# Banded attention beside gated projections: the fourth projection step of every even unit moves behind the second value product

## The chip, the cores and the metric

The kernel runs on one core of one Trainium2 chip. The metric is the device time of one execution in microseconds; the time before is the median of three executions. A core has five engines with a queue of instructions each, and each queue is worked off in the order in which the program wrote it: TensorE (PE, with its weight loads shown apart as PEld), VectorE (DVE), ScalarE (ACT), GpSimd (POOL) and SyncE (SP, here only for DMAs).

## The reference, cut to what matters

One encoder layer of 1024 tokens and 1024 channels. A normalised input is projected; the columns go to two head groups. Group A is banded attention: 8 query heads, 2 key-value heads, and a block of 128 queries sees its own block of keys and the two beside it.

```python
scores = jnp.einsum('bnqgrd,bnkgd->bngrqk', qb, kb).astype(jnp.float32)
scores = scores * (HEAD_DIM ** -0.5)
...
scores = jnp.where(mask[None, :, None, None], scores + bias[None, None], -jnp.inf)
...
m = jnp.maximum(jnp.max(scores, axis=-1, keepdims=True), sink_l)
p = jnp.exp(scores - m)
denom = jnp.sum(p, axis=-1, keepdims=True) + jnp.exp(sink_l - m)
probs = (p / denom).astype(v.dtype)
out = jnp.einsum('bngrqk,bnkgd->bnqgrd', probs, vb)
...
ya = ya * jax.nn.silu(ga)
```

Group B is dense latent attention with its own gate `gb`. Both go through one output projection, a residual sum and a last norm.

## The kernel before, in words

Every engine's program is written out by hand, and semaphores tie them together. The stage around the change is the banded attention, at some 229 to 345 us of the profile. It runs over 16 **units**: unit u is query block n = u // 2 and key-value group g = u % 2, with its four query heads. A loop over s runs from 0 to 16 on each engine; step s works on the scores of unit s and on the value products of unit s - 1 (the text says "unit s" for step s of this loop). The keys of a unit are 3 blocks of 128 (2 blocks for units 0, 1, 14 and 15), called c0, c1 and c2 below.

In step s:

- TensorE makes the scores of unit s (`scores_w`, 8 matmuls, L1601 and L1602, banks 0 to 3), then transposes the probabilities of unit s - 1 for c0 and c1 (`turn_w`, 4 transposes each, L1613, banks 4 and 5), makes the value product of c0 (`pv_w`, 2 matmuls, L1623 and L1624, bank 7), transposes c2, and makes the value products of c1 and c2.
- VectorE takes the negated row maxima of the four heads (`max_w`, L1181), adds the two halves of the output of unit s - 2 (`o_w_sum`, L1219), makes the low part of each transposed block (`pT_w_lo`, L1209), the reciprocal of the sums (`recip_w`, L1195 and L1196), and scales one head's probabilities (`probs_w`, L1203).
- ScalarE copies the lower half of the output (`o_w_lo`, L865), makes the exponentials (`exp_w`, L848, and `exp_sink_w`, L853) and the high part of each transposed block (`pT_w_hi`, L859).
- GpSimd scales the other three heads' probabilities (`probs_w`, L580) and multiplies by the gate (`gate_w`, L591).

Between these, TensorE has work that waits for nothing in this loop: the gated projection jobs. Job g is one 128 x 512 tile of the gate columns, summed over 8 steps; a step k is three matmuls (`three`, L1425 to L1427: high by high, low by high, high by low) into bank 6. `beside(s)` gives each unit four steps of one job: odd units the steps 0 to 3, even units the steps 4 to 7, so that **a job ends in an even unit**. Its last matmul raises `s_g`; ScalarE then takes the tanh from the bank into `Y` (`evac_g`, L841), and VectorE joins the two in `Y` (`evac_g`, L1168). Both stand at the end of step s in their engine's queue, on VectorE right ahead of the first `max_w` of step s + 1:

```python
                if live:
                    probs_w(s)
                if s % 2 == 0:
                    evac_g(N_WIN_JOB + s // 2)
```

A value product waits for `s_wTl`, VectorE's low part of its block (L1209); the scores of a unit wait for the row maxima of the unit before; `max_w` waits for the scores. The first two of the four steps of a unit stand between the transposes and the product of c0; the change is about the other two, "the third" and "the fourth". In even units the fourth is step 7, which ends the job.

Of the kernel before, what the change touches and what calls it, by code (L numbers as in the profile page):

```python
# [71 lines left out]
def encoder(nc, x, norm_mix, w_in, attn_sink, q_a_norm, w_uq, kv_a_norm, w_ukv, w_out, final_norm,  # L72
# [8 lines left out]
    with ExitStack() as ctx:  # L81
# [196 lines left out]
        def beside(s):  # L278


            if s == 0:
                return N_WIN_JOB, range(KT)
            return N_WIN_JOB + (s + 1) // 2, range(4 * ((s + 1) % 2), 4 * ((s + 1) % 2) + 4)
# [4 lines left out]
        def w_keys(u):  # L288
            n = u // GROUPS
            return range(max(n - 1, 0), min(n + 2, NT))  # L290

        W_UNITS = NT * GROUPS
# [1129 lines left out]
        def _(pe):  # L1422
# [155 lines left out]
            def gated(g, ks):  # L1578
                m, cols = g // 2, slice(g % 2 * HALF, (g % 2 + 1) * HALF)
                if ks[0] == 0:  # L1580
                    pe.wait_ge(s_wr, m + 1)
                    if g < 2:
                        wait_up_copied(pe, UP_LAST[g])
                    else:
                        pe.wait_ge(s_ge, g if g > N_WIN_JOB else g - 1)
                for k in ks:
                    last = three(ps[:, g_bank(g), :], w_hi[:, m % 2, k, :], w_lo[:, m % 2, k, :],
                                 hT_hi[:, k, cols], hT_lo[:, k, cols], k == 0, k == KT - 1)
                if ks[-1] == KT - 1:
                    last.then_inc(s_g, 1)  # L1590

            def scores_w(u):
                n, g, keys = u // GROUPS, u % GROUPS, w_keys(u)
                k0, w = keys[0] * P, len(keys) * P
                if u == 0:
                    wait_up_copied(pe, len(UP) - 1)
                for r in range(REP):
                    if u >= 1:
                        pe.wait_ge(s_wm, REP * (u - 1) + r + 1)
                    q = q_st[:, REP * g + r, n * P:(n + 1) * P]  # L1600
                    nc.tensor.matmul(ps[:, r, 0:w], q, k_hi2[:, g, k0:k0 + w], start=True, stop=False)  # L1601
                    nc.tensor.matmul(ps[:, r, 0:w], q, k_lo2[:, g, k0:k0 + w], start=False,  # L1602
                                     stop=True).then_inc(s_ws, 1)

            def turn_w(u, i):
                c = W_FIRST[u] + i
                if i == 0:
                    pe.wait_ge(s_wp, POOL_R * (u + 1))
                    pe.wait_ge(s_wpd, u + 1)
                if c >= 2:  # L1610
                    pe.wait_ge(s_wTl, c - 1)
                for r in range(REP):
                    last = nc.tensor.transpose(ps[:, 4 + c % 2, r * P:(r + 1) * P],  # L1613
                                               p_w[:, u % 2, r, i * P:(i + 1) * P], ident[:, :])
                last.then_inc(s_wT, 1)

            def pv_w(u, i):
                c, keys = W_FIRST[u] + i, w_keys(u)
                if i == 0:
                    pe.wait_ge(s_wo, u) if u else pe.wait_ge(s_ge, N_WIN_JOB)  # L1620
                pe.wait_ge(s_wTl, c + 1)
                v = vA[:, keys[i], u % GROUPS, :]
                nc.tensor.matmul(ps[:, 7, :], v, pT_wh[:, c % 2, :], start=(i == 0), stop=False)  # L1623
                nc.tensor.matmul(ps[:, 7, :], v, pT_wl[:, c % 2, :], start=False,  # L1624
                                 stop=(i == len(keys) - 1)).then_inc(s_wpv, 1)
# [29 lines left out]
            for s in range(W_UNITS + 1):  # L1655
                g, ks = beside(s)
                n = len(w_keys(s - 1)) if s >= 1 else 0
                if s < W_UNITS:
                    scores_w(s)
                if s == W_UNITS:  # L1660
                    gated(g, ks[:len(ks) // 2])
                    ks = ks[len(ks) // 2:]
                for i in range(min(n, 2)):
                    turn_w(s - 1, i)
                if 2 <= s < W_UNITS or s == 0:
                    gated(g, ks[:len(ks) // 2])
                    ks = ks[len(ks) // 2:]
                else:
                    gated(g, ks)
                if n:  # L1670
                    pv_w(s - 1, 0)
                    if n > 2:
                        turn_w(s - 1, 2)
                before = len(ks) if s % 2 == 0 else len(ks) // 2
                if 2 <= s < W_UNITS or s == 0:
                    gated(g, ks[:before])
                if n:
                    pv_w(s - 1, 1)
                if before < len(ks) and s >= 2:
                    gated(g, ks[before:])  # L1680
                if n > 2:
                    pv_w(s - 1, 2)
# [140 lines left out]
```

## Time and profile before

| what | value |
| --- | --- |
| median of three executions | 638.8 us (638.74 to 638.92) |
| the profiled execution, its own time | 639.14 us |
| span of the profiled execution | 636.6 us |
| busy: TensorE matmul / weight load | 626.3 us (98%) / 526.7 us (83%) |
| busy: VectorE / ScalarE / GpSimd | 438.5 us (69%) / 355.4 us (56%) / 315.9 us (50%) |
| mean granted TensorE clock | 0.999 |
| share of TensorE in the chain that ended last | 94% |

The span runs from the first to the last instruction; the device time holds 2.5 us more that lie around it. A matmul's length in the timeline overlaps that of the next, so TensorE's pace is read from the distance of two starts, and its lost time from starts that lie further apart than that. An "idle before" is time in which an engine had nothing, with the instruction that released it behind the arrow.

### The profile page before, as it was taken

How to read it: one execution, taken by the hardware profiler on the slowest of the kernel's cores; microseconds unless marked ns; L12 is line 12 of the kernel's file. 1: busy time of each engine (PE TensorE's matmuls, PEld its weight loads, DVE VectorE, ACT ScalarE, POOL GpSimd, SP SyncE). 2: the span in 40 equal slices, each digit the busy share in tenths (PEclk: the TensorE clock that was granted, in tenths of full speed). 3: DMA queues.
4: the chain of work that ended last, by engine and by line, in shares of the span. 5: the costliest groups of instructions: out<-in, count | busy, mean ns of one | idle time of the engine just before them, and what ended most of it. 6: DMA issues, size and time to landing. Idle time of an engine off the chain costs nothing.

```text
span 636.6 us, 9352 instructions
## 1 busy us (share of the span) xinstructions
PE 626.3 (98%) x3267; PEld 526.7 (83%) x3267; DVE 438.5 (69%) x850; ACT 355.4 (56%) x765; POOL 315.9 (50%) x304
## 2 busy tenths in 40 slices
PE   8999999999999999999999999999999999999996
PEld 7888888888888887888887788888888888888885
DVE  4673326333444448899998788888888888799695
ACT  5662222223333237777776777777777778542563
POOL 2724004404656433644545776877876788610710
PEclk9999999999999999999999999999999999999999
DMA  6540016365676520100015011010010403399033
GB/s 222 188 166 1 1 38 234 134 256 184 227 250 229 190 64 1 34 1 1 10 42 175 0 43 43 1 41 19 24 43 0 141 1 134 108 339 346 0 142 123
DMA packets 41662, 66.80 MB, mean 105 GB/s; under 512 B 3496, under 2 KB 18352, under 8 KB 41488
## 3 DMA queue, kind: packets, MB, share of 16 engines
q1 hardware_dynamic: 41472, 65.95, 31.2%
q8 instruction: 26, 0.43, 0.3%
q10 hardware_dynamic: 144, 0.26, 0.1%
q14 instruction: 20, 0.16, 0.1%
HBM read 46.15 MB, written 20.05 MB: 104 GB/s over the span
## 4 chain that ended last, share of the span: by engine, by line
PE 94%; DVE 2%; ACT 2%; issue 1%; POOL 1%; POOLq 0%; ACTq 0%
PE ps L1427 21%; PE ps L1425 21%; PE ps L1426 21%; PE ps L1696 9%; PE ps L1712 5%; PE ps L1713 5%; PE ps L1613 3%; PE ps L1623 2%; PE ps L1624 1%; PE ps L1437 1%; PE ps L1602 1%; PE ps L1601 1%; PE ps L1477 1%; PE ps L1465 1%; POOL p_w L580 1%
## 5 line engine op out<-in xcount | busy, mean ns | idle before, releaser
L654 POOL TENSOR_SCALAR p_b<-p_b,stat 128x1024 f32<-128x1024 f32 x64 | 72.1, 1126 | 51.2 <-DVE stat L1280 50.7
L928 ACT ACTIVATE pT_hi<-ps 128x512 fp32r<-128x512 f32 x128 | 69.6, 596 | 45.4 <-PE ps L1696 45.4
L1285 DVE TENSOR_TENSOR pT_lo<-ps,pT_hi 128x512 fp32r<-128x512 f32 x128 | 81.8, 680 | 5.2 <-ACT pT_hi L928 5.1
L1275 DVE TENSOR_REDUCE stat<-ps 128x1 f32<-128x1024 f32 x64 | 77.7, 1214 | 10.7 <-PE ps L1427 10.4
L1425 PE MATMUL ps<-hT_hi,w_hi 128*128 128x512 f32 x208 | 83.9, 403 | 0.0
L1427 PE MATMUL ps<-hT_hi,w_lo 128*128 128x512 f32 x208 | 81.4, 391 | 0.0
L1426 PE MATMUL ps<-hT_lo,w_hi 128*128 128x512 f32 x208 | 81.0, 390 | 0.0
L917 ACT ACTIVATE p_b<-ps,stat 128x1024 f32<-128x1024 f32 x64 | 71.5, 1117 | 10.4 <-DVE stat L1275 10.3
L1696 PEld LDWEIGHTS ps<-ident,p_b 128*128 128x128 f32 x512 | 59.9, 141 | 8.9 <-issue 0.5
L1696 PE MATMUL ps<-ident,p_b 128*128 128x128 f32 x512 | 66.5, 273 | 0.1
L580 POOL TENSOR_SCALAR p_w<-p_w,stat 128x384 f32<-128x384 f32 (+1 forms) x48 | 27.8, 596 | 59.5 <-DVE stat L1196 59.5
L1712 PE MATMUL ps<-pT_hi,vB 128*128 128x512 f32 x128 | 55.2, 431 | 0.9 <-DVE Y L1168 0.9
L1713 PE MATMUL ps<-pT_lo,vB 128*128 128x512 f32 x128 | 50.3, 393 | 0.0
L1426 PE MATMUL ps<-k_lo,q_hi 96*128 96x512 f32 x126 | 49.7, 395 | 0.0
L1427 PE MATMUL ps<-k_hi,q_lo 96*128 96x512 f32 x126 | 49.7, 395 | 0.0
L1425 PE MATMUL ps<-k_hi,q_hi 96*128 96x512 f32 x126 | 49.5, 393 | 0.0
L518 POOL TENSOR_SCALAR w_hi<-w_raw 128x1024 fp32r<-128x1024 f32 x13 | 14.1, 1081 | 65.6 <-PE ps L1427 65.6
L1427 PEld LDWEIGHTS ps<-hT_hi,w_lo 128*128 128x128 f32 x208 | 39.0, 188 | 8.4
L1425 PEld LDWEIGHTS ps<-hT_hi,w_hi 128*128 128x128 f32 x208 | 39.1, 188 | 7.5 <-issue 0.4
L1425 PE MATMUL ps<-wn_hi,hT_hi 128*128 128x288 f32 (+1 forms) x128 | 45.1, 352 | 0.0
L1426 PEld LDWEIGHTS ps<-hT_lo,w_hi 128*128 128x128 f32 x208 | 39.2, 188 | 7.1
L1427 PE MATMUL ps<-wn_hi,hT_lo 128*128 128x288 f32 (+1 forms) x128 | 44.1, 344 | 0.0
(219 smaller groups left out, 1525.6 us busy)
## 6 DMA issues: line engine op xcount, KB each, us to landing
w_raw<-w_in SPq DMA_DIRECT2D x13, 512.0 KB, 4.5
x_in<-x SPq DMA_DIRECT2D x8, 512.0 KB, 3.5
wt_raw<-w_out SPq DMA_DIRECT2D x8, 512.0 KB, 4.6
t_scratch<-wt_hi SPq DMA_DIRECT2D x16, 256.0 KB, 2.4
t_scratch<-wt_lo SPq DMA_DIRECT2D x16, 256.0 KB, 2.6
wn_raw<-w_in SPq DMA_DIRECT2D x8, 336.0 KB, 3.5
q_nope_scratch<-stage SPq DMA_DIRECT2D x8, 256.0 KB, 3.1
k_nope_scratch<-stage SPq DMA_DIRECT2D x8, 256.0 KB, 3.3
```

The costliest lines, as they stand in the source:

```text
L580: nc.gpsimd.tensor_scalar(p_w[:, u % 2, r, 0:w], p_w[:, u % 2, r, 0:w], w_col(5, u)[:, r:r + 1], 0.5, ALU.mult, ALU.mult).then_inc(s_wp, 1)
L654: nc.gpsimd.tensor_scalar(p_b[:, (U + 1) % 4, :], p_b[:, (U + 1) % 4, :], r_b[:, U % 4:U % 4 + 1], 0.5, ALU.mult, ALU.mult).then_inc(s_bp, 1)
L917: nc.scalar.activation(p_b[:, (U + 1) % 4, :], ps[:, b:b + 2, :].rearrange("p b c -> p (b c)"), ACT.Exp, bias=nm_b[:, U % 4:U % 4 + 1], ac ...
L928: nc.scalar.activation(pT_hi[:, 1 - G % 2, 4 * a:4 * a + 4, U % 4 * P:(U % 4 + 1) * P], ps[:, 4 + a, :].rearrange("p (k c) -> p k c", c=P) ...
L1275: nc.vector.tensor_reduce(nm_b[:, U % 4:U % 4 + 1], ps[:, b:b + 2, :].rearrange("p b c -> p (b c)"), AX.X, ALU.max, negate=True).then_inc( ...
L1285: nc.vector.tensor_tensor(pT_lo[at_], ps[:, 4 + a, :].rearrange("p (k c) -> p k c", c=P), f(pT_hi[at_]), ALU.subtract).then_inc(s_bTl, 1)
L1425: nc.tensor.matmul(o, a_hi, b_hi, start=first, stop=False, skip_group_check=goes_on)
L1426: nc.tensor.matmul(o, a_hi, b_lo, start=False, stop=False, skip_group_check=goes_on)
L1427: return nc.tensor.matmul(o, a_lo, b_hi, start=False, stop=last, skip_group_check=goes_on)
L1696: last = nc.tensor.transpose(ps[:, 4 + a, k * P:(k + 1) * P], p_b[:, (U + 1) % 4, (4 * a + k) * P:(4 * a + k + 1) * P], ident[:, :])
L1712: nc.tensor.matmul(o, vB[:, 1 - hp, k, :], pT_hi[:, 1 - G % 2, k, :], start=(k == 0), stop=False)
L1713: last = nc.tensor.matmul(o, vB[:, 1 - hp, k, :], pT_lo[:, 1 - G % 2, k, :], start=False, stop=(k == NT - 1))
```

## The change

One expression that says how many of the two remaining gated steps stand ahead of the value product of c1. Before, both in even units and one in odd units; now one in each unit from 2 to 15. Units 0, 1 and 16 keep what they had. No instruction is added or removed, no DMA moves, and the queues of VectorE, ScalarE, GpSimd and SyncE stay as they were, row for row.

```diff
                     pv_w(s - 1, 0)
                     if n > 2:
                         turn_w(s - 1, 2)
-                before = len(ks) if s % 2 == 0 else len(ks) // 2
+                before = len(ks) // 2 if 2 <= s < W_UNITS else len(ks)
                 if 2 <= s < W_UNITS or s == 0:
                     gated(g, ks[:before])
                 if n:
                     pv_w(s - 1, 1)
                 if before < len(ks) and s >= 2:
                     gated(g, ks[before:])
                 if n > 2:
                     pv_w(s - 1, 2)
```

So the fourth step moves in the seven even units 2 to 14. On TensorE in unit 2, where the unit before has two key blocks, the rows are these (k_hi and k_lo by q_st are scores, hT by w the gated step, pT by vA the value product):

```order
 L1426 MATMUL ps<-hT_lo,w_hi 128x512
 L1427 MATMUL ps<-hT_hi,w_lo 128x512
-L1425 MATMUL ps<-hT_hi,w_hi 128x512
-L1426 MATMUL ps<-hT_lo,w_hi 128x512
-L1427 MATMUL ps<-hT_hi,w_lo 128x512
 L1623 MATMUL ps<-pT_wh,vA 128x512 [waits w_pT_lo]
 L1624 MATMUL ps<-pT_wl,vA 128x512
+L1425 MATMUL ps<-hT_hi,w_hi 128x512
+L1426 MATMUL ps<-hT_lo,w_hi 128x512
+L1427 MATMUL ps<-hT_hi,w_lo 128x512
 L1601 MATMUL ps<-k_hi_84,q_st 128x384 [waits w_max]
 L1602 MATMUL ps<-k_lo_85,q_st 128x384
```

The gated step that ended ahead of the product of c1 now ends right ahead of the next unit's scores.

On TensorE in unit 4, and in the same way in units 6, 8, 10, 12 and 14, where the unit before has three key blocks:

```order
 L1426 MATMUL ps<-hT_lo,w_hi 128x512
 L1427 MATMUL ps<-hT_hi,w_lo 128x512
-L1425 MATMUL ps<-hT_hi,w_hi 128x512
-L1426 MATMUL ps<-hT_lo,w_hi 128x512
-L1427 MATMUL ps<-hT_hi,w_lo 128x512
 L1623 MATMUL ps<-pT_wh,vA 128x512 [waits w_pT_lo]
 L1624 MATMUL ps<-pT_wl,vA 128x512
+L1425 MATMUL ps<-hT_hi,w_hi 128x512
+L1426 MATMUL ps<-hT_lo,w_hi 128x512
+L1427 MATMUL ps<-hT_hi,w_lo 128x512
 L1623 MATMUL ps<-pT_wh,vA 128x512 [waits w_pT_lo]
 L1624 MATMUL ps<-pT_wl,vA 128x512
```

The same step, the last of its job, now stands between the products of c1 and c2; the product of c1, with its wait for VectorE, comes three matmuls earlier.

## Rows read from the trace of the kernel before

**Rows 1.** Busy us by engine (and instructions), clock, DMA, 269 to 283 us

```profile
269.00:283.00 14.00, 13.96 (x76) 11.52 (x75) 12.66 (x35) 10.55 (x27) 4.69 (x8) 1.00 0.00 1
```

**Rows 2.** Waits in 228 to 346 us: total us, times, longest

```profile
PEld ps L1623 <- DVE pT_wl L1209: 7.4, 21, 0.6
...
DVE p_w L1181 <- PE ps L1602: 4.1, 7, 0.6
```

**Rows 3.** Timeline of unit 6 (start, length, instruction, idle before)

```profile
269.59 0.62 DVE L1181 CUSTOM_DVE_ANT_0 p_w<-distb,ps,nsink 128x384 f32<-128x384 f32 x1 [0.63 <-PE ps L1602]
...
273.47 0.68 DVE L1209 TENSOR_TENSOR pT_wl<-ps,pT_wh 128x512 fp32r<-128x512 f32 x1
...
274.63 0.40 PE L1427 MATMUL ps<-hT_hi,w_lo 128*128 128x512 f32 x1
...
274.77 0.69 DVE L1209 TENSOR_TENSOR pT_wl<-ps,pT_wh 128x512 fp32r<-128x512 f32 x1
...
274.87 0.39 PE L1623 MATMUL ps<-pT_wh,vA 128*128 128x512 f32 x1
...
275.07 0.60 ACT L841 ACTIVATE Y<-ps 128x512 f32<-128x512 f32 x1 [0.33 <-PE ps L1427]
...
275.52 0.19 PEld L1623 LDWEIGHTS ps<-pT_wh,vA 128*128 128x128 f32 x1 [0.46 <-DVE pT_wl L1209]
...
276.05 0.67 DVE L1168 SCALAR_TENSOR_TENSOR Y<-Y,ps 128x512 f32<-128x512 f32 x1
```

**Rows 4.** Timeline of unit 5

```profile
262.43 0.61 DVE L1181 CUSTOM_DVE_ANT_0 p_w<-distb,ps,nsink 128x384 f32<-128x384 f32 x1
...
263.81 0.60 ACT L859 ACTIVATE pT_wh<-ps 128x512 fp32r<-128x512 f32 x1
...
266.31 0.69 DVE L1209 TENSOR_TENSOR pT_wl<-ps,pT_wh 128x512 fp32r<-128x512 f32 x1
...
267.05 0.19 PEld L1623 LDWEIGHTS ps<-pT_wh,vA 128*128 128x128 f32 x1 [0.29 <-DVE pT_wl L1209]
...
268.08 0.40 PE L1427 MATMUL ps<-hT_hi,w_lo 128*128 128x512 f32 x1
...
268.36 0.19 PEld L1623 LDWEIGHTS ps<-pT_wh,vA 128*128 128x128 f32 x1 [0.31 <-DVE pT_wl L1209]
```

**Rows 5.** Timeline of unit 8

```profile
287.90 0.68 DVE L1209 TENSOR_TENSOR pT_wl<-ps,pT_wh 128x512 fp32r<-128x512 f32 x1
...
288.96 0.39 PE L1427 MATMUL ps<-hT_hi,w_lo 128*128 128x512 f32 x1
...
289.39 0.60 ACT L841 ACTIVATE Y<-ps 128x512 f32<-128x512 f32 x1 [0.34 <-PE ps L1427]
...
290.36 0.67 DVE L1168 SCALAR_TENSOR_TENSOR Y<-Y,ps 128x512 f32<-128x512 f32 x1
```

**Rows 6.** Timeline from unit 2 into unit 3

```profile
245.51 0.68 DVE L1209 TENSOR_TENSOR pT_wl<-ps,pT_wh 128x512 fp32r<-128x512 f32 x1
...
246.25 0.40 PE L1427 MATMUL ps<-hT_hi,w_lo 128*128 128x512 f32 x1
...
246.69 0.60 ACT L841 ACTIVATE Y<-ps 128x512 f32<-128x512 f32 x1 [0.39 <-PE ps L1427]
...
247.32 0.69 DVE L1168 SCALAR_TENSOR_TENSOR Y<-Y,ps 128x512 f32<-128x512 f32 x1 [0.16 <-ACT Y L841]
...
249.48 0.60 ACT L859 ACTIVATE pT_wh<-ps 128x512 fp32r<-128x512 f32 x1 [0.20 <-PE ps L1613]
...
250.11 0.69 DVE L1209 TENSOR_TENSOR pT_wl<-ps,pT_wh 128x512 fp32r<-128x512 f32 x1 [0.16 <-ACT pT_wh L859]
```

**Rows 7.** Timeline of unit 14

```profile
330.09 0.68 DVE L1209 TENSOR_TENSOR pT_wl<-ps,pT_wh 128x512 fp32r<-128x512 f32 x1
...
331.88 0.60 ACT L841 ACTIVATE Y<-ps 128x512 f32<-128x512 f32 x1 [0.60 <-PE ps L1427]
...
332.51 0.69 DVE L1168 SCALAR_TENSOR_TENSOR Y<-Y,ps 128x512 f32<-128x512 f32 x1
```

## Prediction

> **What bounds the kernel now.** I read the busy time of the banded stage first. Of 14 us in its middle TensorE shows 13.96 busy, VectorE 12.66, ScalarE 10.55 and GpSimd 4.69, at a granted clock of 1.00 [rows 1]. TensorE looks like the bound, but its matmuls overlap in the records, so I went on to the waits: in this stage 21 weight loads of a value product waited for VectorE's low part, and in turn 7 row maxima waited for TensorE's scores [rows 2]. Two engines that wait for each other form a ring, and the question is which pieces of it have no slack.
>
> The timeline of a pair of units answers it. In unit 5 VectorE starts its first maximum at 262.43 with no idle time ahead of it, because it came straight from other work [rows 4]; in unit 6 the first maximum at 269.59 waited 0.63 us for the scores [rows 3]. So the ring is: VectorE's maxima of an odd unit, by way of ScalarE's exponentials and high parts, to the low part of c2; TensorE's product of c2 at 268.36, which waited for just that [rows 4]; the scores of the even unit; VectorE's even unit without a gap worth naming; `evac_g` at 276.05; the next odd unit's maxima. TensorE is on it only from 268.36 to 269.59. Inside an even unit it runs beside the ring, and VectorE's `evac_g` is on it. That is the place to price.
>
> A rule of the Trainium skill bears on this choice. By Perfetto Trace Analysis, Identifying the Most-Contended Engine, matmul busy time is a bad measure, and weight-load busy time is to be set against VectorE's occupancy. Here that is 11.52 us against 12.66 [rows 1], so by the rule VectorE is the engine to guard, where the matmul row alone would name TensorE; by the rule I would go with the forecast below, by the matmul row with the first rival.
>
> **What the change moves.** Nothing is added or removed; three matmuls of 0.23 us pace change places with two, seven times. Two things follow in an even unit: the product of c1 comes three matmuls earlier and may now wait for its low part; and the last matmul of the job, on which ScalarE's tanh and then VectorE's `evac_g` wait, comes later.
>
> *Units 6 and 10.* The low part of c1 ends at 273.47 + 0.68 = 274.15 [rows 3]. TensorE would be there at 274.63 - 2 x 0.23 = 274.17, so they meet almost exactly. Unit 5 is already laid out in the new way and gives the price: low part ends at 266.31 + 0.69 = 267.00, the load follows at 267.05, and the last matmul of the fourth step starts at 268.08, thus 1.03 us behind the load [rows 4]. (At full pace these four distances would be 0.92; 0.11 is a weight load that nothing covers.) In unit 6 that makes load 274.20 and last matmul 275.23, where it was 274.63 [rows 3]: 0.60 later.
>
> ScalarE's tanh starts 0.44 behind that matmul and takes 0.60, and `evac_g` could begin 0.03 later (246.69 + 0.60 to 247.32 in rows 6), at 275.70. It began at 276.05, since VectorE was busy until then [rows 3]: 0.35 us of cover. So 0.60 - 0.35 = **0.25 us** reach VectorE. TensorE itself loses nothing: after 275.23 it is at the product of c2 at 275.46, and the low part of c2 ends at 274.77 + 0.69 = 275.46, load 275.51, as before [rows 3].
>
> *Units 4, 8 and 12.* Here the low part of c1 comes a little later: 287.90 + 0.68 = 288.58, load 288.63, last matmul 289.66 where it was 288.96, 0.70 later. The cover is 290.36 - (289.39 + 0.60 + 0.03) = 0.34, which leaves **0.36** [rows 5]. The same arithmetic on unit 4 gives 0.34 and on unit 12 0.36.
>
> *Unit 2.* The unit before has two key blocks, so there is no product of c2 to meet, and VectorE has no third low part. c1's low part ends at 245.51 + 0.68 = 246.19, load 246.24, last matmul 247.27 where it was 246.25: 1.02 later. There is no cover: `evac_g` already waited 0.16 for the tanh. In unit 3 ScalarE had 0.20 to spare ahead of its first high part, and VectorE's low part waits for that one, so 1.02 - 0.20 = **0.82** goes on [rows 6]. Bounds: the scores of unit 3 come 247.27 + 0.23 - (246.25 + 3 x 0.23) = 0.56 later in any case, which is the least; 1.02 is the most.
>
> *Unit 14.* The low part of c1 ends at 330.77, and TensorE comes there no earlier (tanh at 331.88, so the last matmul at 331.44, less 2 x 0.23) [rows 7]. So the step is later by two matmuls alone, 0.46. `evac_g` at 332.51 stood 0.03 behind the tanh's end at 332.48, without cover [rows 7]: **0.46**.
>
> *What waits behind `evac_g`.* On VectorE all maxima of the odd unit, its output sum and its low parts; behind the first maximum ScalarE's first exponential and, in its queue, the high part of c0; behind the low parts TensorE's products. In unit 5 the high part of c0 runs 263.81 to 264.41 and the load of c1's product stood 0.29 and that of c2's 0.31 for VectorE [rows 4]; I see no slack in between that would eat 0.25 us. The 0.63 us that VectorE waits in the even unit [rows 3] is no slack either: it waits for scores that TensorE makes after the late product, so it waits as long as before. No DMA is issued by the moved step, and bank 6 is needed again only behind the next unit's scores and transposes. GpSimd's last weight splits wait for jobs that ended over a unit ago.
>
> **The sum**: 0.82 + 0.34 + 0.25 + 0.36 + 0.25 + 0.36 + 0.46 = 2.84 us, on the profiled execution 639.14 + 2.84 = 641.98. That execution lies 0.34 over the median of 638.8, so I forecast 641.6 us for the median, 0.44% slower. The dense stage behind starts later by the same amount, and I take it that it gives nothing back: its first scores follow on TensorE without a pause.
>
> Bounds of what the trace does not show. Each of the five middle units could cost nothing (if VectorE's odd unit has slack that I missed) or 0.36 (the larger of the two). If the ring swallows all five, units 2 and 14 stay: 0.82 + 0.46 = 1.28, thus 640.1. Upwards: unit 2 in full 1.02, five at 0.36, unit 14 0.46, and on top in all seven an uncovered weight load of 0.11: 3.28 + 0.77 = 4.05, thus 642.8.
>
> **Rivals.**
>
> *TensorE is the bound, and the moved step fills its wait: faster.* The product of c2 in the five middle units waits: its load at 275.52 stands 0.19 behind the pace (274.87 + 2 x 0.23 = 275.33) [rows 3], and with the uncovered load of 0.11 that is 0.30 lost. The new order puts a step into it and pays 0.03 + 0.11 at the product of c1, so 0.16 would be saved five times: 0.8 us, 638.0. For it speaks the 13.96 of 14 us. Against it: the low part of c2 hangs on the exponentials, not on TensorE's matmuls of that moment, so the product can't start sooner; it decides only if that low part came 0.16 us earlier. I give it 0.05.
>
> *Swallowed: no change.* The later `evac_g` would be absorbed by slack in the odd unit, and unit 2 too. The idle times in rows 4 speak against it. 639 to 640: 0.09.
>
> *Only the ends count.* The middle units meet their cover, units 2 and 14 cost: 640.1, on the border of what can be told. 0.10.
>
> *TensorE pays too.* The wait for c1 is longer than reckoned, so that the product of c2 is late as well, by 0.11 each time or more: 642.4 and above. 0.08.
>
> *The forecast*, 641.0 to 642.3: 0.68.
>
> **Numbers.** About 0.2% (1.3 us) is what a measurement of this kernel can tell from no change. Slower than 640.1 are the forecast, the last rival and half of "only the ends": 0.81. Same: the swallowed case, half of the ends: 0.14. Faster: 0.05. The range of 8 in 10 takes in the ends and part of the bounds: 640.1 to 642.6.
>
> **What would show it.** In the changed profile: (1) in unit 6 a load of the product of c1 that waits for L1209 and starts 0.05 behind its end, and none longer than before at c2; (2) the tanh of unit 6 starting 1.52 us behind the end of the low part of c1 (275.67 against 274.15); (3) `evac_g` in all seven even units with a wait for ScalarE's tanh ahead of it, 0.25 to 0.36 in the middle; (4) the distance from one even unit's first maximum to the next 0.25 to 0.36 us longer than now; (5) the first scores of the dense stage 2.8 us later. The forecast is wrong if (3) holds and (4) does not: then the odd unit has slack. It is also wrong if the wait at c1 is longer than at unit 5.

## The result, and the profile after

The changed kernel takes 640.83 us (median of 6 runs, 640.20 to 641.15) against 638.76 us for the kernel before (6 runs, 637.81 to 638.92): ratio 1.0035, 95% interval 1.0025 to 1.0045. It is 2.07 us slower. The forecast was 641.6 us with a range of 640.1 to 642.6. The profiled execution spans 638.4 us, 1.8 more than before. Its banded stage began 0.5 us earlier than that of the profile before, so the loss within the stage is 2.3 us.

The busy times of the whole span tell nothing of it: TensorE's matmuls rose from 626.3 to 627.9 us and its weight loads fell from 526.7 to 526.0. Nor does the same stretch of 14 us as in [rows 1]:

```profile
269.00:283.00 14.00, 14.00 (x76) 11.48 (x76) 12.51 (x35) 10.56 (x27) 4.57 (x8) 1.00 0.00 1
```

TensorE now shows 14.00 of 14 us busy, and the kernel is slower. The waits of the banded stage (total us, times, longest; to be laid beside [rows 2]) say more:

```profile
ACT Y L841 <- PE ps L1427: 15.2, 10, 4.8
...
DVE Y L1168 <- ACT Y L841: 10.2, 10, 4.8
...
PEld ps L1623 <- DVE pT_wl L1209: 9.4, 27, 0.7
```

Before, the wait of `evac_g` for the tanh was this:

```profile
DVE Y L1168 <- ACT Y L841: 7.5, 4, 4.8
```

TensorE's loads waited for VectorE's low parts 27 times instead of 21, and 9.4 us instead of 7.4. ScalarE's tanh waited 15.2 us for the jobs' last matmuls instead of 10.5. VectorE's `evac_g` waited 10 times for the tanh instead of 4: all seven changed units now wait, by 1.18, 0.26, 0.17, 0.24, 0.17, 0.28 and 0.57 us, where only unit 2 did before. VectorE's wait for scores is the old one (4.1 us, 7 times). The delay comes back to TensorE one unit later: ahead of the loads of value products the view shows 3.1 us of idle time without a releaser ("issue"), 0.4 before, and all but 0.2 of it stands at the product of c0 in the odd units.

Unit 6 and the start of unit 7 after the change (start, length, instruction, idle before), to be laid beside [rows 3]:

```profile
270.20 0.62 DVE L1181 CUSTOM_DVE_ANT_0 p_w<-distb,ps,nsink 128x384 f32<-128x384 f32 x1 [0.62 <-PE ps L1602]
...
274.09 0.68 DVE L1209 TENSOR_TENSOR pT_wl<-ps,pT_wh 128x512 fp32r<-128x512 f32 x1
...
274.82 0.19 PEld L1623 LDWEIGHTS ps<-pT_wh,vA 128*128 128x128 f32 x1 [0.29 <-DVE pT_wl L1209]
...
275.85 0.40 PE L1427 MATMUL ps<-hT_hi,w_lo 128*128 128x512 f32 x1
...
276.29 0.60 ACT L841 ACTIVATE Y<-ps 128x512 f32<-128x512 f32 x1 [0.93 <-PE ps L1427]
...
276.92 0.69 DVE L1168 SCALAR_TENSOR_TENSOR Y<-Y,ps 128x512 f32<-128x512 f32 x1 [0.17 <-ACT Y L841]
...
277.52 0.60 DVE L1181 CUSTOM_DVE_ANT_0 p_w<-distb,ps,nsink 128x384 f32<-128x384 f32 x1
```

The low part of c1 ends at 274.09 + 0.68 = 274.77 and the load follows at 274.82. The last matmul of the job starts 1.03 behind it, at 275.85, the tanh at 276.29, and `evac_g` has waited 0.17 us. The first maximum stands 0.60 behind `evac_g`, and 0.30 behind the end of its scores (276.88 + 0.34 = 277.22). So `evac_g` holds the maximum, and not the scores. Nor is it ScalarE's own queue that hands the delay on, for its next exponential waits 0.67 us for that maximum. Counted from the unit's first maximum, `evac_g` starts at 6.72 us; before it was 276.05 - 269.59 = 6.46. The forecast said 0.25 later, and it is 0.26. But the unit 7 that follows is only 0.16 later.

The first maximum (first L1181) of each unit, counted from that of unit 0, gives the whole account. Before, it stands at 230.04, 269.59 and 276.75 for units 0, 6 and 7, after at 229.57, 270.20 and 277.52; "dense" is the first matmul of the dense scores (L1640; 343.12 and 344.96). What the change added by then, in us:

| at unit | 3 | 4 | 5 | 6 | 7 | 8 | 9 | 10 | 11 | 12 | 13 | 14 | 15 | dense |
| --- | --- | --- | --- | --- | --- | --- | --- | --- | --- | --- | --- | --- | --- | --- |
| after less before | 1.03 | 0.84 | 1.09 | 1.08 | 1.24 | 1.25 | 1.49 | 1.49 | 1.66 | 1.66 | 1.93 | 1.94 | 2.33 | 2.31 |

All steps stand at odd units, right behind the `evac_g` of a changed unit, and between an odd and the next even unit nothing is added; at unit 4 the spare time of unit 3 is given back, as forecast.

### The profile page after: what moved, and what is told of

Same layout as the page of the kernel before. It is cut to its first block, busy times and chain, and to the rows that moved or that the text cites. A ratio compares the mean times of both kernels' runs of the same rounds, so it can differ in the third digit from the quotient of the medians.

```text
span 638.4 us, 9352 instructions
## 1 busy us (share of the span) xinstructions
PE 627.9 (98%) x3267; PEld 526.0 (82%) x3267; DVE 438.8 (69%) x850; ACT 355.8 (56%) x765; POOL 316.6 (50%) x304
## 4 chain that ended last, share of the span: by engine, by line
PE 94%; DVE 3%; ACT 1%; issue 0%; POOL 0%; POOLq 0%; ACTq 0%
PE ps L1425 21%; PE ps L1427 21%; PE ps L1426 21%; PE ps L1696 9%; PE ps L1712 5%; PE ps L1713 5%; PE ps L1613 3%; PE ps L1623 2%; PE ps L1624 1%; PE ps L1602 1%; PE ps L1601 1%; PE ps L1437 1%; PE ps L1477 1%; DVE p_w L1181 1%; DVE pT_wl L1209 1%; PE ps L1465 1%
## 5 line engine op out<-in xcount | busy, mean ns | idle before, releaser
L1275 DVE TENSOR_REDUCE stat<-ps 128x1 f32<-128x1024 f32 x64 | 77.7, 1214 | 10.5 <-PE ps L1427 10.3
L848 ACT ACTIVATE p_w<-p_w,stat 128x384 f32<-128x384 f32 (+1 forms) x64 | 37.4, 585 | 12.0 <-DVE stat L1181 10.8
```

What stands on the lines that cost most here:

```text
L848: nc.scalar.activation(p, p, ACT.Exp, bias=w_col(0, u)[:, r:r + 1], scale=-1.0, accum_out=w_col(3, u)[:, r:r + 1])
L1275: nc.vector.tensor_reduce(nm_b[:, U % 4:U % 4 + 1], ps[:, b:b + 2, :].rearrange("p b c -> p (b c)"), AX.X, ALU.max, negate=True).then_inc( ...
```

## The experiments

Each run is told by its median beside that of the kernel before, which ran beside it on the same chip, and by the length of its banded stage in the profile: from unit 0's first maximum to the first dense score matmul, 113.08 us before and 115.39 after. The stage is the sharper measure, since it leaves out how the other 525 us of an execution vary, but it is read from one profiled execution of each kernel. "Late release" is the theory of the prediction: the job ends later, so VectorE's `evac_g` does, and it stands ahead of the odd unit's maxima. The rival "TensorE's own loss" says that each changed unit pays at its second wait, whatever VectorE does.

### The change in unit 2 alone

```diff
-                before = len(ks) if s % 2 == 0 else len(ks) // 2
+                before = len(ks) if s % 2 == 0 and s != 2 else len(ks) // 2
```

> The fourth step stands behind the product of c1 in unit 2 alone; units 4 to 14 are as before. Late release (the job ends later, so VectorE's evac_g and the next first maximum start later): the trace of the full change has 0.83 us between unit 2 and unit 4, so the time is 0.8 us over before, and the first maximum of unit 4 is 0.83 later against the start of unit 2. TensorE's own loss (each changed unit pays one more uncovered wait, 2.1 us over seven units): 0.3 us over before.

639.24 us against 638.26, ratio 1.0010 (1.0001 to 1.0019). The stage is 113.98 us, 0.90 more; at unit 3 the first maximum is 1.06 later, at unit 4 0.87, and from there to the end it stays at 0.86 to 0.90. So unit 2 alone carries over a third of the loss. Late release, with its 0.8, holds; the equal share of 0.3 does not. (The 0.8 of this expectation was read from the profile of the full change; what the run adds is that unit 2 does it by itself.)

### The change in the five middle units alone

```diff
-                before = len(ks) if s % 2 == 0 else len(ks) // 2
+                before = len(ks) if s % 2 == 0 and s not in range(4, 13) else len(ks) // 2
```

> The fourth step stands behind the product of c1 in units 4, 6, 8, 10 and 12 alone. Late release: 0.24 + 0.17 + 0.24 + 0.17 + 0.28 = 1.1 us over before, with the larger steps in units 4, 8 and 12 and each step at the first maximum of the following odd unit. TensorE's own loss: five times 0.3, 1.5 us over before, equal in the five units.

639.35 us against 638.26, ratio 1.0016 (1.0007 to 1.0025). Stage 114.22 us, 1.14 more. The steps at units 5, 7, 9, 11 and 13 are 0.27, 0.14, 0.28, 0.17 and 0.26 us: the larger ones behind units 4, 8 and 12, as in the full change. The two parts and unit 14 add up to within 0.12 us: 0.90 + 1.14 leave 0.27 of the 2.31 for unit 14, where the step at unit 15 reads 0.39.

### The mirror: both steps ahead in the odd units too

```diff
-                before = len(ks) if s % 2 == 0 else len(ks) // 2
+                before = len(ks)
```

> The mirror of the change: both remaining steps stand ahead of the product of c1 in the odd units too, where the moved step does not end a job. Late release: nothing hangs on that step, and the product of c2 waits for VectorE's low part as before, so the time is that of before within 0.3 us, and the waits at c1 in the odd units are gone without a gain. TensorE's own loss: seven waits at c1 with an uncovered load of 0.14 us in all are saved, 1.0 us faster.

638.70 us against 638.26, ratio 1.0005 (0.9996 to 1.0013). The waits of loads for low parts in the stage:

```profile
PEld ps L1623 <- DVE pT_wl L1209: 6.0, 14, 0.6
```

Seven waits at c1 are gone (14 instead of 21), and nothing is won: the first maximum of unit 14 stands 0.11 us later than before. The place of the step in an odd unit, where it ends no job, is worth next to nothing, and an uncovered load (one that no running matmul hides) costs nothing ahead of a product whose successor waits anyway. The stage as a whole is 0.43 us longer, and 0.31 of that comes behind unit 15. There the unit before has two key blocks, so the product of c1 is the last one; it now stands three matmuls later in the queue and its load starts 0.53 us later, and ScalarE's low half of the output, VectorE's sum and the first high part of the dense stage's operands, all behind it, start 0.42 later. I had not seen that: the expected 0.3 us is missed by this end piece, while the units before it hold to it.

### Without the tanh, both orders

Neither ScalarE's tanh nor the gate of the seven jobs is computed; VectorE's `evac_g` keeps its place and size, but waits for the last matmul itself. The first `evac_g` below is ScalarE's, the second VectorE's.

```diff
             def evac_g(g):
+                if N_WIN_JOB < g < N_WIN_JOB + 8:
+                    return
...
             def evac_g(g):
-                dve.wait_ge(s_ga, g + 1)
+                direct = N_WIN_JOB < g < N_WIN_JOB + 8
+                if direct:
+                    dve.wait_ge(s_g, g + 1)
+                else:
+                    dve.wait_ge(s_ga, g + 1 if g <= N_WIN_JOB else g - 6)
...
-                    last = nc.vector.scalar_tensor_tensor(out=Y[:, m - 5, cols], in0=Y[:, m - 5, cols],
+                    src = f(hT_hi[:, m - 5, cols]) if direct else Y[:, m - 5, cols]
+                    last = nc.vector.scalar_tensor_tensor(out=Y[:, m - 5, cols], in0=src,
```

> The order of before; in the seven jobs that end in units 2 to 14 ScalarE's tanh is left out and VectorE's evac_g waits for TensorE's last matmul itself (it multiplies the bank by other data of the same size, so the gate of these jobs is not computed). It is the base for the run beside it. Late release: evac_g of the middle units was not waiting and the first maximum waits for the scores, so only unit 2 may gain (up to 0.2): the stage from unit 0's first maximum to the first dense scores stays at 113.1 us (113.08 before), and the time within 0.3 us of before. TensorE's own loss: no change either.

> The same, without the tanh of the seven jobs, in the order of after. Late release: the job ends 0.6 later but VectorE could take it 0.6 earlier, so the middle units and unit 14 cost nothing and only unit 2 stays (the scores of unit 3 are 0.56 later, less what unit 3 has to spare): 0.2 to 0.6 us over the run beside it in the stage. TensorE's own loss at the two waits: it is untouched by what VectorE waits for, so the difference between the two orders stays at 2.1 to 2.3 us.

638.39 us in the order of before against 638.42 for the kernel before (ratio 1.0003, 0.9994 to 1.0012) and 638.60 us in the order of after (0.9998, 0.9989 to 1.0008): neither can be told from the kernel before, nor from each other. The stages are 113.17 and 113.41 us, so the order that costs 2.31 us there costs 0.24 here. At unit 3 the difference is 0.67, at unit 4 it is 0.24, and it stays between 0.20 and 0.24 up to the dense stage: units 4 to 14 cost nothing at all. Unit 6 of the new order without the tanh (the lines of this kernel are shifted by 7: L1216 is a low part, L1434 the last matmul of a step, L1630 the load of a product, L1175 `evac_g`, L1188 a maximum):

```profile
273.80 0.68 DVE L1216 TENSOR_TENSOR pT_wl<-ps,pT_wh 128x512 fp32r<-128x512 f32 x1
...
274.54 0.19 PEld L1630 LDWEIGHTS ps<-pT_wh,vA 128*128 128x128 f32 x1 [0.30 <-DVE pT_wl L1216]
...
275.57 0.39 PE L1434 MATMUL ps<-hT_hi,w_lo 128*128 128x512 f32 x1
...
276.37 0.67 DVE L1175 SCALAR_TENSOR_TENSOR Y<-hT_hi,ps 128x512 f32<-128x512 f32 x1
...
277.08 0.61 DVE L1188 CUSTOM_DVE_ANT_0 p_w<-distb,ps,nsink 128x384 f32<-128x384 f32 x1
```

TensorE waits at c1 as with the tanh, its load starting 0.06 behind the end of the low part, and its last matmul comes 1.03 later. Only VectorE no longer waits: in units 4 to 14 `evac_g` has no idle time ahead of it. In unit 2 it still waits 0.57 us, now for the last matmul itself, and there the 0.24 come from. This tells the two theories apart, since TensorE's waits at c1 and c2 and their uncovered loads are all there (27 waits, 9.0 us, against 9.4 with the tanh) and the loss is not. What went with the tanh is TensorE's waiting at c0 ("issue" 0.6 us instead of 3.1), which was the delay handed on.

### Early scores, both orders

TensorE issues the scores of the next unit's first head ahead of the product of c2 instead of behind it, at the end of units 3 to 13.

```diff
-                    scores_w(s)
+                    scores_w(s, range(1, REP) if 4 <= s < W_UNITS - 1 else range(REP))
...
+                if 3 <= s < W_UNITS - 2:
+                    scores_w(s + 1, range(1))
                 if n > 2:
                     pv_w(s - 1, 2)
```

> The order of before, and the scores of the next unit's first head are issued ahead of the product of c2, at the end of units 3 to 13. If TensorE's way from the product of c2 to the first scores is part of the ring (it is what 0.62 us of VectorE's wait in even units and the first maximum of odd units, 0.10 us behind the end of evac_g, say), the first maximum of an even unit follows VectorE's probs_w at once and that of an odd unit stands 0.60 behind the start of evac_g. VectorE's ring of 14.31 us a pair loses up to 0.72, TensorE's rows give 0.60 back at most, so some 0.5 in five or six pairs: 2.5 to 3.5 us faster than before. If the scores are not on the ring: no change.

> Scores of the next unit's first head ahead of the product of c2 (at the end of units 3 to 13), in the order of after. In the order of before this stage took 111.54 us. If the price of the change was 0.55 us under the sum because the first maximum of an odd unit waited 0.10 us for the scores as well, that cover is gone here in the five middle units, and the change costs 0.82 + 1.56 + 0.39 = 2.8 us against early_scores_old_order: stage 114.3 us. If the shortfall came from elsewhere, it costs 2.3 again: 113.8.

In the order of before: 637.02 us against 638.26, ratio 0.9974 (0.9964 to 0.9985). It is faster than both kernels of this study. The stage is 111.54 us, 1.54 less; I had hoped for 2.5 to 3.5. Units 6 and 7 of it:

```profile
268.49 0.62 DVE L1181 CUSTOM_DVE_ANT_0 p_w<-distb,ps,nsink 128x384 f32<-128x384 f32 x1
...
275.41 0.67 DVE L1168 SCALAR_TENSOR_TENSOR Y<-Y,ps 128x512 f32<-128x512 f32 x1
...
276.00 0.60 DVE L1181 CUSTOM_DVE_ANT_0 p_w<-distb,ps,nsink 128x384 f32<-128x384 f32 x1
```

The first maximum of the even unit follows `probs_w` with no idle time, and that of the odd unit stands 0.59 behind `evac_g`, where before it was 0.70. So the scores had been holding both. What took their place is a wait of VectorE's output sum for ScalarE's low half, 0.36 us in each of units 4, 6, 8, 10 and 12. Over the stage it was 0.9 us, 2 times, before and is now this (the second row is what is left of the wait for scores):

```profile
DVE o_w L1219 <- ACT ol_w L865: 3.2, 8, 0.6
...
DVE p_w L1181 <- PE ps L1602: 0.5, 1, 0.5
```

In the order of after: 640.65 us, ratio to the kernel before 1.0031 (1.0020 to 1.0042). The stage is 115.02 us, so the change costs 3.48 us on top of early scores. That is more than either number that I gave (2.8 and 2.3). By units the difference of the two profiles grows by 0.29 and 0.26 behind units 6 and 10, where the full change had cost 0.16 and 0.17: the 0.10 us of cover (time by which `evac_g` could be later without harm) that lay in the scores is gone there, as the first of the two cases said. Behind units 8 and 12 it grows by 0.50 and 0.51 against a forecast of 0.36, and behind unit 4 by 0.82, of which 0.14 are given back by unit 6.

In unit 4 two things add up. Early scores brought VectorE 0.62 us forward and the tanh only 0.14, so that with the old order the tanh ends at 261.17 and `evac_g` starts at 261.21: the cover was used up. And the shift is larger than 0.70. Counted from the unit's first maximum, the last matmul of the job comes 0.83, 0.85 and 0.84 us later by the new order in units 4, 8 and 12 (0.62 and 0.60 in units 6 and 10). Less the cover of 0.01, 0.37 and 0.35 us (what lay between the tanh's end and `evac_g` with the old order, without the usual 0.03) this is 0.82, 0.48 and 0.49, so nothing much is left open.

Why these three units shift more can be read from a small sum on VectorE right ahead of the low part of c1 (L1189, 128x4). It takes 0.16 to 0.17 us in the other units from 1 to 15. In units 4, 8 and 12 GpSimd makes the low part of a weight meanwhile (L520), and the sum ends when GpSimd does. Unit 8 with early scores in the old order:

```profile
284.79 2.41 POOL L520 TENSOR_TENSOR w_lo<-w_raw,w_hi 128x1024 fp32r<-128x1024 f32 x1
...
286.80 0.41 DVE L1189 TENSOR_TENSOR stat<-stat,nsink 128x4 f32<-128x4 f32 x1
```

284.79 + 2.41 = 287.20 and 286.80 + 0.41 = 287.21. In the kernel before the sum takes 0.26 to 0.27 us in these units, and ends with GpSimd too; these 0.10 us are why the low part of c1 comes later there, and why the forecast was 0.36 in them and 0.25 in units 6 and 10. No run takes GpSimd's work away, so that it is the cause rests on the ends alone, which meet within 0.03 us in these three units of all ten kernels of this study.

### Early scores, and the output sum one maximum later

```diff
                 if live:
                     max_w(s, 0)
-                if s >= 2:
-                    o_w_sum(s - 2)
                 if live:
                     max_w(s, 1)
+                if s >= 2:
+                    o_w_sum(s - 2)
```

> The order of before with the early scores, and VectorE's o_w_sum stands behind the second maximum instead of behind the first. In early_scores_old_order VectorE waited 8 times, 3.2 us in all, for ScalarE's low half of the output there; if that wait is what took the place of the wait for scores, it goes and the stage falls from 111.54 to about 110.0 (0.3 us in each of five even units), bounded by TensorE's rows without waits. If TensorE or ScalarE's exponentials set the pace now: no change, 111.5.

636.73 us against 638.42, ratio 0.9976 (0.9966 to 0.9985), and a stage of 111.55 us: no better than early scores alone (111.54). The wait for ScalarE's low half is gone from the list, and another has grown:

```profile
DVE pT_wl L1209 <- ACT pT_wh L859: 3.5, 9, 0.7
```

VectorE now waits 9 times, 3.5 us in all, for ScalarE's high part of a transposed block; with early scores alone it was 2 times and 0.9 us. The wait that had looked like the next limit only stood in front of one of the same size.

## Why the prediction was right, and where it was off

**The order of the bound.** That VectorE's `evac_g` and the maxima behind it, not TensorE's fill, decide the price, held: without the tanh, the same order of matmuls costs 0.24 us in the stage instead of 2.31. The rival by which the moved step fills TensorE's wait is refuted by the measured time, and its saving is not there in any unit: in unit 6 the load of c2's product still starts 0.05 us behind the low part it waits for (275.39 + 0.69 = 276.08, load 276.13). The Trainium skill (Perfetto Trace Analysis, Identifying the Most-Contended Engine) says that matmul busy time does not tell how near the limit TensorE is, and names weight-load busy time instead. The trace agrees on the first: the matmul row rose from 13.96 to 14.00 of 14 us while the kernel got slower. On the second it says little, since the loads went from 11.52 to 11.48 us.

**Unit 2**: forecast 0.82, measured 0.84 at unit 4 (0.86 to 0.90 alone). The evacuation was 1.02 later in the forecast; the first maximum of unit 3 is 1.03 later. The rows after show how it came about:

```profile
247.88 0.69 DVE L1168 SCALAR_TENSOR_TENSOR Y<-Y,ps 128x512 f32<-128x512 f32 x1 [1.18 <-ACT Y L841]
...
248.48 0.61 DVE L1181 CUSTOM_DVE_ANT_0 p_w<-distb,ps,nsink 128x384 f32<-128x384 f32 x1
```

The maximum stands 0.60 behind `evac_g`, which waits for the tanh. At unit 4 0.2 are given back by what ScalarE had to spare: its high part of c0 no longer waits (0.20 before) and starts 1.37 us behind the unit's first maximum instead of 1.56. The least that the prediction gave, 0.56 because the scores of unit 3 are later "in any case", is no floor: without the tanh these scores are later by as much, and only 0.24 reach unit 4.

**Units 4 to 12**: forecast 0.34, 0.25, 0.36, 0.25, 0.36, together 1.56; measured at the next odd unit 0.25, 0.16, 0.24, 0.17, 0.27, together 1.09. The shift of `evac_g` came out to 0.01 us in four of the five units and to 0.03 in unit 8, that of the last matmul to 0.03 or better. Mis-sized was the term "0.35 us of cover": I took the cover to end where `evac_g` started. But the first maximum of unit 7 was not waiting for `evac_g` alone. Before the change:

```profile
276.26 0.34 PE L1602 MATMUL ps<-k_lo,q_st 128*128 128x384 f32 x1
...
276.75 0.61 DVE L1181 CUSTOM_DVE_ANT_0 p_w<-distb,ps,nsink 128x384 f32<-128x384 f32 x1
```

The first head's scores end at 276.26 + 0.34 = 276.60, and the maximum follows 0.15 later, at 276.75; behind a wait for scores it does so everywhere (as at 269.59 in [rows 3], whose scores are not shown). By `evac_g`, which started at 276.05, it could have begun 0.60 later, at 276.65. So 0.10 us more of cover lay in the scores, and the profile shows no idle time for it, since it fell within the recorded length of `evac_g`. My sentence that TensorE is on the ring only from 268.36 to 269.59 was wrong by this much: it was on it in both kinds of units, and `evac_g` was not. Five times some 0.09 are 0.47 of the missing 0.53 us. Early scores took this piece away and the maximum moved to 0.59 behind `evac_g`.

**Unit 14**: forecast 0.46, measured 0.39. The same cause. Before the change the first head's scores of unit 15 end at 332.76 + 0.28 = 333.04, the maximum starts 0.14 later, at 333.18, where `evac_g` would have let it begin at 332.51 + 0.60 = 333.11: 0.07 of cover.

**What waits behind it.** That the odd unit swallows nothing, and that the 0.63 us of VectorE's wait in the even unit are no slack, held: the table gives nothing back between units 4 and 15. Of the five signs named in advance three came as described: the wait at c1 as in unit 5 and none longer at c2, the tanh 1.52 behind the low part (274.77 to 276.29), a wait for the tanh ahead of `evac_g` in all seven units (but 0.17 to 0.28 in the middle ones, not 0.25 to 0.36, because it is counted from the recorded end of VectorE's instruction before). The other two came in kind but short in size. The distance from one even unit's first maximum to the next grew by 0.24, 0.17, 0.24, 0.17 and 0.28 us, where 0.25 to 0.36 was said, and the dense scores start 2.31 us later within the stage, where 2.8 was said: both by the mis-sized cover. The time of the whole execution is 2.07 over that before; the 0.2 between these two is within what the runs vary, and that the median lies still further below the forecast of 641.6 than the stage does is chance.

## What to carry to other kernels

When a step is moved, ask first what it releases, and price that: three matmuls that ended a job cost 2 us by their place, and the place of the same step in the odd units, where it ends nothing, is worth 0.1 us at most up to unit 14. The cover of a wait (how much later its releaser may come) is measured not to the start of the next instruction but to the last of all its releasers, also of the one behind it; a wait of 0.1 us that falls within a record's length shows no idle time. And an engine shown as fully busy, with waits filled by moved work, can belong to a slower kernel: look for the ring of waits and its slack, then fill.

## What the runs showed of the hardware

A VectorE maximum started 0.14 to 0.15 us behind the modelled end of the scores that released it, in units 6, 7 and 15 of the kernel before, but only 0.60 us behind the start of an `evac_g` of 0.67 to 0.69 us: records of one queue overlap by some 0.07 to 0.09 us, so a wait of that size leaves no trace as idle time.

While GpSimd made a 128x1024 subtraction of 2.4 us (L520), a VectorE sum of 128x4 elements that had begun meanwhile took 0.26 to 0.52 us instead of 0.16, and ended within 0.03 us of GpSimd's end (units 0, 4, 8 and 12 of the kernel before; the delay is read from the ends that meet, and no run without GpSimd's work was made).
